# Expert products of a mixture-of-experts decoder block in plain fp32, with twelve one-megabyte weight buffers

## What is computed

```
def expert_block(args):
    e, toks, g = args
    xb = jnp.take(xt, toks, axis=0, mode='clip')
    hdn = xb @ w_up[e] + b_up[e]              # 1024 -> 2048
    h_gate, h_lin = jnp.split(hdn, 2, axis=-1)
    h_gate = jnp.minimum(h_gate, SWIGLU_LIMIT)
    h_lin = jnp.clip(h_lin, -SWIGLU_LIMIT, SWIGLU_LIMIT)
    act = (h_lin + 1.0) * (h_gate * jax.nn.sigmoid(SWIGLU_ALPHA * h_gate))
    y = act @ w_down[e] + b_down[e]           # 1024 -> 1024
    return y * g[:, None].astype(y.dtype)
```

## Time and profile before

| what | value |
|---|---|
| median of 3 runs | 1738.14 us |
| span of the profiled execution | 1738.5 us |
| TensorE (PE) busy | 1668.7 us (96%) |
| VectorE (DVE) busy | 1502.9 us (86%) |
| ScalarE (ACT) busy | 1062.2 us (61%) |
| HBM read | 454.15 MB |

### The profile page before, as it was taken

The page is one execution under the profiler, slowest core; times in us unless marked ns, Lnnn a source line. Parts: engine busy times, 40 slices in busy tenths (PEclk is TensorE's granted clock), DMA queues, the critical chain, the costliest instruction groups (busy, mean ns, idle before and its releaser), DMA issues.

```text
span 1738.5 us, 22182 instructions
## 1 busy us (share of the span) xinstructions
PE 1668.7 (96%) x7129; PEld 1088.9 (63%) x7129; DVE 1502.9 (86%) x1689; ACT 1062.2 (61%) x1015; POOL 466.9 (27%) x298
## 2 busy tenths in 40 slices
PE   4999999999998999999999999999999999999996
PEld 2333344466576577777777777777777777777763
DVE  5999886656667899999999999999999999999995
ACT  4323212266444577777777777777777777777771
POOL 4864200074533021122222121212222121211210
PEclk9998999999998999999999999999999999999997
DMA  5111113110407999999999999999999999999973
GB/s 174 49 52 49 49 49 121 49 69 30 142 37 263 375 353 361 361 364 376 366 368 362 372 377 355 370 357 376 368 363 360 373 376 365 365 361 377 378 277 106
DMA packets 91902, 464.76 MB, mean 267 GB/s; under 512 B 21290, under 2 KB 21406, under 8 KB 42617
## 3 DMA queue, kind: packets, MB, share of 16 engines
q1 hardware_dynamic: 80240, 441.67, 66.7%
q0 software_dynamic: 9776, 18.41, 4.3%
q10 hardware_dynamic: 1848, 4.24, 0.7%
HBM read 454.15 MB, written 18.53 MB: 272 GB/s over the span
## 4 chain that ended last, share of the span: by engine, by line
PE 83%; DVE 12%; issue 2%; ACT 1%; DMA 1%; POOL 1%; ACTq 0%; DVEq 0%; POOLq 0%
PE ps L1778 19%; PE ps L1780 19%; PE ps L1779 19%; PE ps L1571 6%; PE ps L1764 3%; DVE w_lo L1205 2%; PE ps L1498 2%; PE ps L1479 2%; PE ps L1493 2%; PE ps L1786 2%; PE ps L1487 1%; PE ps L1680 1%; PE ps L1681 1%; PE ps L1682 1%; DVE scr L1065 1%
## 5 line engine op out<-in xcount | busy, mean ns | idle before, releaser
L1205 DVE TENSOR_TENSOR w_lo<-raw,w_hi 128x2048 fp32r<-128x2048 f32 x384 | 873.7, 2288 | 73.1 <-ACT w_hi L838 71.9
L838 ACT ACTIVATE w_hi<-raw 128x2048 fp32r<-128x2048 f32 x384 | 737.0, 1919 | 239.1 <-PE ps L1780 237.8
L1778 PE MATMUL ps<-w_hi,x_hi 128*96 128x512 f32 x1024 | 414.1, 404 | 0.0
L1780 PE MATMUL ps<-w_lo,x_hi 128*96 128x512 f32 x1024 | 403.0, 394 | 0.0
L1779 PE MATMUL ps<-w_hi,x_lo 128*96 128x512 f32 x1024 | 402.2, 393 | 0.0
L1778 PEld LDWEIGHTS ps<-w_hi,x_hi 128*96 128x96 f32 x1024 | 168.2, 164 | 67.0 <-issue 2.0
L1778 PE MATMUL ps<-w_hi,a_hi 128*96 128x512 f32 x512 | 204.7, 400 | 5.7 <-DVE a_lo L1316 5.7
L1780 PEld LDWEIGHTS ps<-w_lo,x_hi 128*96 128x96 f32 x1024 | 165.3, 161 | 70.8
L1779 PEld LDWEIGHTS ps<-w_hi,x_lo 128*96 128x96 f32 x1024 | 165.9, 162 | 63.9
L605 POOL DMA_INDIRECT gate_now<-gate_rows,row_now x32 | 79.8, 2495 | 455.0 <-DVE tok_out L1346 439.9
L1779 PE MATMUL ps<-w_hi,a_lo 128*96 128x512 f32 x512 | 201.9, 394 | 0.0
(11 more groups left out here) (325 smaller groups left out, 2002.5 us busy)
## 6 DMA issues: line engine op xcount, KB each, us to landing
raw<-in_w_up SPq DMA_DIRECT2D x256, 1024.0 KB, 8.2
raw<-in_w_down SPq DMA_DIRECT2D x128, 1024.0 KB, 10.6
ring<-in_w_in SPq DMA_DIRECT2D x9, 2048.0 KB, 7.8
ring<-in_w_glu SPq DMA_DIRECT2D x4, 1024.0 KB, 6.2
ring<-in_w_o SPq DMA_DIRECT2D x2, 2048.0 KB, 11.7
h<-in_x SPq DMA_DIRECT2D x4, 512.0 KB, 5.6
ring<-in_w_attn_proj SPq DMA_DIRECT2D x1, 2048.0 KB, 8.1
h_rows<-h ACTq DMA_DIRECT2D x4, 512.0 KB
```

The lines of the kernel that those rows point to most:

```text
L838: s.activation(hi_of(c)[:, :], raw_of(c), ACT.Copy).then_inc(s_hi, 1)
L1205: d.tensor_tensor(lo_of(c)[:, :], raw_of(c), hi_of(c)[:, :], ALU.subtract).then_inc(s_lo, 1)
L1778: mm(o, xh, hi_of(c)[:, col], start=start, stop=False)
L1780: return mm(o, xh, lo_of(c)[:, col], start=False, stop=stop)
```

## The change

The halves are gone. TensorE multiplies the loaded part itself by the transposed tokens, both plain fp32, in one product for each 512-column piece; it waits for the load of the part (`s_raw`) where it waited for its split. ScalarE's L838 and VectorE's L1205 and L1316 are removed, and ScalarE copies the transposes (`keep_T`). `raw` has twelve buffers. SP loads a buffer again when TensorE has used it (`s_cu`), issues the first 12 parts at once, and the loads of block 0 ahead of the table of experts. The load of `slots` moves from SP's queue to GpSimd's. The number of blocks is read as a remainder and 31 is added to it.

```
-NRAW, NSPLIT = 6, 4
+NRAW = 12
...
-            def product(o, xh, xl, c, w, stop, start=False):
-                col = slice(w, w + 512)
-                mm(o, xh, hi_of(c)[:, col], start=start, stop=False)
-                mm(o, xl, hi_of(c)[:, col], start=False, stop=False)
-                return mm(o, xh, lo_of(c)[:, col], start=False, stop=stop)
+            def part_in(t, c):
+                pe.wait_ge(s_raw[(AHEAD + c) % NRAW], (t + (AHEAD + c) // NRAW) * 16 + 16)
...
-                pe.wait_ge(s_lo, part_no(t, c) + 1)
+                part_in(t, c)
                 for n in range(4):
-                    ins = product(ps[n][0:BLK, :], x_hi[:, p, :], x_lo[:, p, :], c, 512 * n, p == KD - 1)
+                    ins = mm(ps[n][0:BLK, :], xT[:, p, :], raw_of(c)[:, 512 * n:512 * n + 512], start=False,
+                             stop=p == KD - 1)
                 ins.then_inc(s_cu, 1)
...
             sp.wait_ge(s_wo, 2 * TT)
             for p in range(8):
-                if p >= NRAW:
-                    sp.wait_ge(s_lo, p - NRAW + 1)
                 up(-1, p + 4, 0, p)
-            sp.wait_ge(s_scat, 16 * TT * TOPK)
-            sp.dma_start(slots[:, 0:NE], first_list.rearrange("(p b) o -> p (b o)", p=BLK)).then_inc(s_slots, 16)
+            for c in range(PARTS):
+                if part_no(0, c) >= NRAW:
+                    sp.wait_ge(s_cu, part_no(0, c) - NRAW + 1)
+                if c < 8:
+                    up(0, c, 1, c)
+                else:
+                    down(0, c, 0, c - 8)
...
             for t in range(TT):
                 write_first(t)
+            pool.wait_ge(s_scat, 16 * TT * TOPK)
+            g.dma_start(slots[:, 0:NE], first_list.rearrange("(p b) o -> p (b o)", p=BLK)).then_inc(s_slots, 16)
             pool.wait_ge(s_h1row, 16 * TT)
             gather(1)
...
-            def T_hi(dst, half, job, bank):
+            def keep_T(dst, half, job, bank):
                 act.wait_ge(s_tr, job + 1)
                 s.activation(dst[:, 4 * half:4 * half + 4, :].rearrange("p k t -> p (k t)"), ps[bank][:, 0:4 * BLK],
-                             ACT.Copy).then_inc(s_thi, 1)
+                             ACT.Copy).then_inc(s_tk, 1)
```

More of the change, by code:

```diff
@@ L235, in build @@
         raw = over("raw", [P, NRAW, PART], F32, at_ring)
[L237 to L241, removed]
+        xT, aT = over("x_T", [P, KD, BLK], F32, at_u), over("a_T", [P, KD, BLK], F32, at_v)
         act_s = far[0:BLK, 0:2, :]
@@ L455, in _ @@
             for p in range(8):
-                if p >= NRAW:
-                    sp.wait_ge(s_lo, p - NRAW + 1)
                 up(-1, p + 4, 0, p)
-            sp.wait_ge(s_scat, 16 * TT * TOPK)
-            sp.dma_start(slots[:, 0:NE], first_list.rearrange("(p b) o -> p (b o)", p=BLK)).then_inc(s_slots, 16)
-            sp.wait_ge(s_tab, 1)
[L463 to L469, removed]
+            for c in range(PARTS):
[5 more added lines that the diff above has]
+                    down(0, c, 0, c - 8)
+            sp.wait_ge(s_tab, 1)
+            final = sp.snap(sp.value_load(etab_i[0:1, NB:NB + 1], min_val=0, max_val=BTAIL - 1) + (NE - 1))
+            turns_left = sp.snap(final - 1)
+            with sp.Fori(0, turns_left) as i:
+                now = sp.value_load(etab_i[0:1, bass.ds(i + 1, 1)], min_val=0, max_val=NE - 1)
+                later = sp.value_load(etab_i[0:1, bass.ds(i + 2, 1)], min_val=0, max_val=NE - 1)
                 for c in range(PARTS):
-                    sp.wait_ge(s_lo, part_no(i, c) - NRAW + 1)
+                    sp.wait_ge(s_cu, i * PARTS + (part_no(1, c) - NRAW + 1))
                     if c < 8:
-                        up(i, c, later, c)
+                        up(i + 1, c, later, c)
                     else:
-                        down(i, c, now, c - 8)
+                        down(i + 1, c, now, c - 8)
             now = sp.value_load(etab_i[0:1, bass.ds(final, 1)], min_val=0, max_val=NE - 1)
             for c in range(4):
-                sp.wait_ge(s_lo, part_no(final, c) - NRAW + 1)
+                sp.wait_ge(s_cu, part_no(final, c) - NRAW + 1)
                 down(final, c, now, c)
@@ L832, in _ @@
                 s.activation(mix_hi[:, i, :], mixT[:, i, :], ACT.Copy).then_inc(s_mixhi, 1)
[L833 to L838, removed]
             second, third = slice(NE, 2 * NE), slice(2 * NE, 3 * NE)
@@ L888, in _ @@
             keep_hT1(3)
-            hi(-1, 4)
             gate_exps(3)
-            hi(-1, 5)
-            def T_hi(dst, half, job, bank):
+            def keep_T(dst, half, job, bank):
                 act.wait_ge(s_tr, job + 1)
                 s.activation(dst[:, 4 * half:4 * half + 4, :].rearrange("p k t -> p (k t)"), ps[bank][:, 0:4 * BLK],
-                             ACT.Copy).then_inc(s_thi, 1)
+                             ACT.Copy).then_inc(s_tk, 1)
             for half in range(2):
-                T_hi(x_hi, half, half, 2 + half)
+                keep_T(xT, half, half, 2 + half)
             for r, nm in enumerate(("ln2_g", "ln2_b")):
                 act.dma_start(gb[:, r, :], a[nm][0].partition_broadcast(P)).then_inc(s_gb3, 16)
-            hi(-1, 6)
             act.wait_ge(s_gts, TT)
@@ L914, in sigm @@
                     s.activation(sig[half], ps[half][0:BLK, :], ACT.Sigmoid, scale=SWI).then_inc(s_sig, 1)
-            for c in range(7, 15):
-                hi(-1, c)
             sigm(-1, 11)
-            hi(-1, 15)
             for half in range(2):
-                T_hi(x_hi, half, 2 + half, 6 + half)
+                keep_T(xT, half, 2 + half, 6 + half)
             def blk(i):
[L925 to L930, removed]
+                for half in range(2):
+                    keep_T(aT, half, i * 4 + 4 + half, 6 + half)
                 sigm(i, 7)
-                hi(i, 11)
                 for half in range(2):
-                    T_hi(x_hi, half, i * 4 + 6 + half, 6 + half)
-                for c in range(12, 15):
-                    hi(i, c)
+                    keep_T(xT, half, i * 4 + 6 + half, 6 + half)
                 y_back(i, 11)
-                hi(i, 15)
             def y_back(t, c):
@@ L953, in _ @@
             for half in range(2):
-                T_hi(a_hi, half, final * 4 + 4 + half, 6 + half)
+                keep_T(aT, half, final * 4 + 4 + half, 6 + half)
             y_back(final, 3)
@@ L1311, in sums @@
                                            bank[:, :], ALU.mult, ALU.add).then_inc(s_gbf, 1)
[L1313 to L1316, removed]
             def swiglu(t, c):
@@ L1350, in _ @@
             pick_expert(0)
-            for half in range(2):
-                T_lo(x_lo, x_hi, half, half, 2 + half)
             first_addresses(TT - 1, TT)
-            lo(-1, 5)
-            lo(-1, 6)
             tables()
[L1357 to L1368, removed]
+            final = dve.snap(dve.value_load(etab_i[0:1, NB:NB + 1], min_val=0, max_val=BTAIL - 1) + (NE - 1))
+            dve.wait_ge(s_slots, 16)
+            next_token(1)
+            dve.wait_ge(s_h1row, 16 * TT)
+            for t in range(TT - 1):
+                sums(t)
             pick_expert(1)
             swiglu(-1, 11)
-            for half in range(2):
-                T_lo(x_lo, x_hi, half, 2 + half, 6 + half)
             sums(3)
-            lo(-1, 15)
             def blk(i):
                 next_token(i + 2)
[L1379 to L1384, removed]
                 next_row(i)
-                lo(i, 10)
                 swiglu(i, 7)
[L1388 to L1391, removed]
                 pick_expert(i + 2)
-                for c in range(13, 16):
-                    lo(i, c)
             for i in range(TT):
@@ L1410, in _ @@
                 assert step.n == PER
-            for half in range(2):
-                T_lo(a_lo, a_hi, half, final * 4 + 4 + half, 6 + half)
             next_row(final)
@@ L1760, in T4 @@
             def T4(cols, job, bank):
-                pe.wait_ge(s_tlo, job - 1)
+                pe.wait_ge(s_tk, job - 1)
                 for k in range(4):
@@ L1799, in down_part @@
                         kk = 2 * p + k
-                        ins = product(ps[4 + r][0:BLK, :], a_hi[:, kk, :], a_lo[:, kk, :], c, DFF * k + 512 * r,
-                                      kk == KD - 1, start=kk == 0)
+                        w = DFF * k + 512 * r
+                        ins = mm(ps[4 + r][0:BLK, :], aT[:, kk, :], raw_of(c)[:, w:w + 512], start=kk == 0,
+                                 stop=kk == KD - 1)
                 ins.then_inc(s_cu, 1)
@@ L1818, in blk @@
                     down_part(i, c, c - 8)
-            pe.wait_ge(s_tlo, 2)
+            pe.wait_ge(s_tk, 2)
             pe.wait_ge(s_b3, 1)
```

23 lines of the change are left out of this document (7 added, 16 removed).

## The result

The changed kernel takes 1983.58 us, the median of 4 runs (1981.45 to 1989.96), against 1738.4 for the kernel before (4 runs): a ratio of 1.141, 95% interval 1.139 to 1.143. The forecast was 1992, slower, with a range of 1979 to 2025. One execution of the later run two_products took 5721.67 us and is left out of its median; every other execution lies within 0.4% of the median of its kernel.

A forecast was written before the change was run, and what follows sets the result against it. TensorE's own work was taken to fill each 35.73 us block, with loads, ScalarE and VectorE keeping up. 1738.5 + 253.5 (product) + 4.0 (start) - 4.0 (end) = 1992.0 us; range for 8 in 10: 1979 to 2025.

The forecast's parts named there:

- The product: Experts' blocks: two plain fp32 records of 0.4309 us replace three of 0.2305; 43.91 us a block, +253.5 us over 31 blocks.
- The upper bound of this term: Experts' blocks: each plain record might pay 0.015 us more, per start or for busy memory; 1.4 us a block, +45.
- The loads: Weight loads in the blocks: hidden with twelve buffers or six, at 299 GB/s; cost 0.
- two resources run full: Middle of the kernel before: TensorE without a gap, DMA queues at 367 GB/s and share 0.98; the timeline must decide.
- Inside the blocks: Blocks: ScalarE's 12 copies and VectorE's 12 splits go, both hidden; 0.
- The start: Start of the experts, up to block 0: +4.0 us, between +0 and +12.
- The wait that was named as late next: Ahead of block 0: TensorE waits for the activation, shorter than the 4.24 us before; block 0 at 586.2, +2.0 us.
- The 2 us for a late gather: Ahead of block 0: slots list lands 8.3 us later on GpSimd's queue, delaying the first gather; 0 to some 10, nearest 2.
- The end: Behind the last block: TensorE goes on 4.3 us earlier, products cost +0.3; sum -4.0 us, between -5 and 0.
- (a): Experts' blocks: a plain record is dearer than in the gate tiles, starts over 0.445 apart; +68, about 2060 us; chance 7%.
- (b): Experts' blocks: a product is one record and the loads decide; about 1590 to 1604 us, faster than before; chance 2%.
- (c): Start of the experts: list, slots and gather land late, TensorE waits 12 to 20 us; about 2005 to 2012; chance 6%.

The follow-up runs named there:

- two_products: Kernel before with two products of three (w_hi by x_hi and by x_lo), VectorE's split left out: 1656.2 us, ratio 0.953.
- products_alone: Kernel before with only the product changed to plain fp32 on the loaded part, six buffers and all splitting kept: 1990.1 us, ratio 1.145.
- six_buffers: Changed kernel with six weight buffers instead of twelve: 1980.6 us, ratio 1.138 to the kernel before.
- small_loads_after: Changed kernel with loads inside the loop over blocks moving 64 of 2048 columns of each part: 1982.3 us, one run.
- small_loads_before: Kernel before with loads inside the loop over blocks moving 64 of 2048 columns of each part: 1740.2 us, one run.
- grouped: Kernel before with the twelve products of a part reordered so that neighbours share the stationary side: 1738.8 us, ratio 0.999.
- one_product: Kernel before with one product of three (x_hi and w_hi), VectorE's split left out: 1657.9 us, ratio 0.952.

## Why the prediction was right

**The product, the term that decided.** "Two for each product ... 0.4309 each": two records held, and 0.4293 came for 0.4309; the block's other 2.54 us are 43.72 - 96 x 0.4293 = 2.51. Forecast 43.91 us a block, measured 43.72; +253.5 forecast, +247.7 measured. The error of this term is 5.8 us, and 4.8 of them are the 1.6 ns on a record (96 x 31 of them). products_alone shows that this term alone makes the change of the blocks. The forecast of 1992 lies 2 us above the profiled execution and 8 above the median; the profiled execution is the slowest of the four.

**The upper bound of this term** was 0.015 us more a record, +45 us, for starts or for busy memory. It was needless: with memory quiet the fp32r records still start 0.23 us apart and the changed kernel's blocks stay, so the surplus of a fp32r record is not the memory, and a plain record has no such surplus. It widened the range by some 22 us.

**The loads**, cost 0 with twelve buffers or six: shown by six_buffers and small_loads_after. 299 GB/s were forecast and 300 measured; the share was 0.87 and not near 0.8. The prediction said "two resources run full" of the kernel before and let the timeline decide for TensorE; small_loads_before confirms it by experiment.

**Inside the blocks**, removal of splits and copies 0: shown, by the equal blocks of products_alone.

**The start**, +4.0 forecast, +5.9 measured in the profiled execution. Four pieces differ. (1) The forecast took 1.0 us off for the removed x_lo, which is the length of the two subtractions; the wait that they caused was 0.60 us, so no more than that could go. (2) TensorE began at 547.58 and not at 545.65: the front part of the program, which the change hardly touches, ended at other times in each kernel profiled (the bias products start at 541.5 to 547.6 in the ten traces). (3) From there to block 0 it is 42.5 us; the forecast had 586.2 - 545.65 = 40.6. The 24 records from 560.18 to 573.34 took 13.16 us where 24 x 0.4293 are 10.30; the granted clock of this stretch says why:

```profile
555.90:560.20 4.30, 4.30 (x10) 1.42 (x9) 0.00 (x0) 0.00 (x0) 0.19 (x1) 0.84 1.25 360
560.20:573.30 13.10, 13.10 (x25) 4.67 (x24) 2.71 (x6) 0.00 (x0) 2.60 (x4) 0.79 0.95 374
```

The clock fell after the eight gated-bias records of 32 rows, although TensorE had no gap. In the kernel before, the products behind them ran at 1.00. The prediction took the slow clock of the start over as a constant, and this step failed, by 2.9 us. It is no property of the changed kernel, though. In grouped, a kernel with the products of before, the clock fell to 0.50 at the same place (552.8 to 558.1). And six_buffers and small_loads_after issue the same products here, and the same 24 records took 12.17 and 10.47 us.

```profile
555.52 12.24 PE L1718 MATMUL ps<-raw,x_T 128*96 128x512 f32 x24
567.69 1.98 PE L1689 MATMUL ps<-scr 32*128 32x512 f32 x4
...
556.58 10.54 PE L1718 MATMUL ps<-raw,x_T 128*96 128x512 f32 x24
567.05 1.98 PE L1689 MATMUL ps<-scr 32*128 32x512 f32 x4
```

In small_loads_after, where the loads of this stretch are whole, the clock stayed at 1.00 over these records, and from the first bias product to block 0 it is 583.79 - 543.43 = 40.4 us, as forecast. So the clock here differs from one execution to the next, and a start that came out within 2 us of the forecast is in part luck. What makes it fall stays open. The wait that was named as late next (the activation) came out at 1.72 us, against 1.8 by the prediction's sum (586.2 - 584.4). (4) The 2 us for a late gather were wrong the other way: TensorE did not wait for the rows at 582.19. GpSimd's load of the slots landed in 6.0 us and not in 10.6:

```profile
slots<-first_list POOLq DMA_DIRECT2D x1, 12.0 KB, 6.0
...
567.31 1.02 POOL L586 DMA_INDIRECT scr<-h_rows,tok_now  x1 [6.71 <-DVE tok_now L1298]
```

The first gather went out 6.0 us later than before, and the forecast had 8.3.

**The end**, -4.0 forecast, -4.0 measured. Its parts hold too: from the transposes to the products 1947.86 - 1945.42 = 2.44 us where it was 6.74, with a wait of 1.35 us for 5.66, and 1961.66 - 1947.86 = 13.80 us for the products where 13.79 was expected, at the full clock.

**The rivals.** (a) a dearer record in the experts (starts over 0.445): 0.4293, out. (b) one record for a product: 3072 records for 1536 products, out. Had it held, the loads would have set the time, and one_product is the nearest run to that: 1657.9 us and not 1590 to 1604, since the loads sustained 391 GB/s there and 417 was a peak of ten microseconds. (c) a start late by 12 us or more: out, it came 5.9 us later.

The Trainium skill halves the array's rate for its fp32 low/high form ("Perfetto Trace Analysis", Engine Utilization). Half the rate is what one of the two records shows here, 0.4293 us for 512 columns; the plain fp32 product is two of them, 0.859 us, a quarter of the rate. The same section gives 358 GB/s as a core's share of the memory while both cores of a pair use it, and lets a lone core pull more, up to about 435 GB/s from its DMA engines. The trace agrees: one core sustained 391 GB/s in one_product.

## What to carry to other kernels

A split into upper and lower halves costs three records of 0.2305 us, a plain fp32 product two of 0.4293: three are cheaper than the one instruction by 0.17 us, as long as another engine can make the halves beside TensorE. Before work is taken off an engine, ask whether the engine that fills the block gets anything from it; 1600 us of busy time went from VectorE and ScalarE here for some 7 us at the end (products_alone against the changed kernel). A DMA share near 1 does not prove a bound: shrink the loads and look whether the time moves. That the time stays says nothing on how far the loads are from the bound; here they were 2.5 us a block behind it.

## What was not expected of the hardware

A fp32r record of 512 columns starts 0.2305 us after the one before in the mean of the experts' blocks, 17 ns over its 512 columns at one column a clock of 2.4 GHz. A plain fp32 record starts every 0.4293 us, only 2.6 ns over twice that time (0.4267 us). The surplus of the fp32r record does not go with another order of the products or with quiet memory, and it is not the same everywhere: 13 ns in the second part of a block and in the output projection, 18 in the products of w_down. What it is stays open.

GpSimd's issue of an indirect DMA waits for a split that VectorE has begun. In products_alone, VectorE's splits and GpSimd's gathers:

```profile
1159.25 2.29 DVE L1205 TENSOR_TENSOR w_lo<-raw,w_hi 128x2048 fp32r<-128x2048 f32 x1 [0.62 <-ACT w_hi L838]
1159.49 2.92 POOL L597 DMA_INDIRECT scr<-h_rows,tok_now  x1 [2.95 <-DVE tok_now L1340]
...
1181.38 0.98 POOL L605 DMA_INDIRECT gate_now<-gate_rows,row_now  x1 [18.96 <-DVE tok_out L1346]
1181.43 2.29 DVE L1205 TENSOR_TENSOR w_lo<-raw,w_hi 128x2048 fp32r<-128x2048 f32 x1 [0.86 <-ACT w_hi L838]
```

The first gather starts inside a split and ends 0.87 us behind the split's end; the second starts just ahead of one and takes 0.98 us. The other gathers of token rows and of gate weights between 700 and 1480 us of this trace fall into the same two kinds. The gather of token rows is 2189 ns in the mean on the page before, 2724 in products_alone, and 993 to 996 in every kernel without splits, with loads of 391 GB/s or of 36. With the splits and small loads it is 2169. The page after:

```profile
L586 POOL DMA_INDIRECT scr<-h_rows,tok_now x32 | 31.8, 995 | 19.1 <-issue 9.1
```

GpSimd was off the path in both kernels.
